# Expert stage of a two-layer decoder trunk: blocks of 1792 columns, 7 KB pieces and eight raw tiles in place of blocks of 896, 3.5 KB pieces and six

## The chip, the core and the metric

The kernel runs on one core of one Trainium2 chip. The metric is the device time of one execution in microseconds. TensorE does the matrix products, ScalarE (ACT) and VectorE (DVE) the element-wise work, GpSimd (POOL) some of the routing and the indirect transfers, and SyncE (SP) issues the loads of the weights. Sixteen DMA engines move the data.

## What is computed

Two decoder layers on 256 tokens of width 1024, all in float32. The first has a gated convolution beside windowed attention, then a dense SwiGLU. The second has block attention (with 256 tokens it is causal attention on one block), then an expert SwiGLU: eight experts with 3584 hidden columns, each token sent to two. Both end with a per-layer embedding. The change is in the expert stage:

```python
def swiglu(x, w_gate, w_up, w_down):
    return (jax.nn.silu(x @ w_gate) * (x @ w_up)) @ w_down

def moe_swiglu(x, w_router, w_gate, w_up, w_down):
    logits = (x @ w_router).astype(jnp.float32)
    top_vals, top_idx = lax.top_k(logits, TOP_K)
    top_w = jax.nn.softmax(top_vals, axis=-1)
    gates = jnp.sum(jax.nn.one_hot(top_idx, N_EXPERTS, dtype=jnp.float32) * top_w[..., None], axis=-2)
    out = jnp.zeros_like(x)
    for e in range(N_EXPERTS):
        out = out + gates[..., e:e + 1].astype(x.dtype) * swiglu(x, w_gate[e], w_up[e], w_down[e])
    return out
```

An expert has three matrices of 1024 x 3584 floats, 14.68 MB each, so that the stage reads 8 x 3 x 14.68 = 352 MB.

## The kernel before

Experts are handled in pairs ("duos"), four of them with these inputs. Of a duo one job is **wide** (up to 128 tokens) and one **small** (up to 64). The wide job's products are made of three: its weights and its inputs are split into a high part in float32r and the rest, and TensorE adds high x high, high x low and low x high. ScalarE makes the high part of a weight tile (`w_hi`, L1096), VectorE the low one (`w_lo`, L2486), so a wide tile passes through both before TensorE has it. The small job uses the raw float32 tile as it was loaded, and since its result has only 64 rows, two products lie side by side on the two halves of the array (`tile_position`).

**Tiles and slots.** SyncE loads weight tiles into `raw`, six slots of up to 1 MB, one after the other in a fixed order, and waits for the slot's last reader ahead of each (`slot_free`): of a wide tile that is VectorE's low part (`lo_made`), of a small one TensorE's products (`tile_used`). There are four `w_hi` buffers and three `w_lo` buffers. L421 is the line of all these loads.

**Blocks.** The 3584 hidden columns are worked in four blocks of 896 (`CUT`). A step of 24 tiles has, in this order of tile numbers: four gate tiles of the wide job (0 to 3), its four up tiles (4, 6, 8, 9) with two down tiles of the small job's last block between them (5, 7), the small job's gate tiles (10, 11, 13, 15) with its other down tiles (12, 14), and then in turn four down tiles of the wide job (16, 18, 20, 22) and four up tiles of the small one (17, 19, 21, 23). A gate or up tile holds two of the eight 128-row slices of the matrix, 896 columns of each: every partition gets two pieces of 896 x 4 = 3584 bytes, 896 KB in all. A down tile holds 256 rows, and a partition gets two neighbouring rows, one piece of 8192 bytes; the fourth of a block has 128 rows and pieces of 4096.

**Folding.** In a small gate or up tile the two slices are computed on the two array halves (L1839). So the two halves of the result are partial sums that have to be added: ScalarE copies both out (L1116, L1120), TensorE transposes them (`turn_sums`, L1798, seven transposes each for gate and up), ScalarE copies the one part (L1125, L1130), VectorE adds the other (L2504, L2510), and only then come Silu (L1135) and the product (L2516). The small down products (L1887) also have two partial sums, which `fold_y` adds once a duo; the sums stand in two PSUM banks, cleared by VectorE. The wide job's hidden values are transposed with seven transposes a block (`turn_wide`, L1788), split into `hidT_hi` (L1112) and `hidT_lo` (L2498), and used by `wide_down` (L1852) in two banks that `clear_wide` clears.

**Order.** Each engine's order is written out by hand. On ScalarE that is `block`, `second_half`, `final_half`; on VectorE `block`; on TensorE `first_half`, `second_half`, `final_half`; on SyncE `superstep`. Silu of the wide gate sums (L1107) stands on ScalarE behind the splits of tiles 4 and 6, the first two up tiles, once gate tile 3 is used, and the copy of the turned hidden values (L1112) ahead of the split of the first down tile.

**Opening and end.** The first expert's gate and up tiles for the wide job can be loaded before the routing is known; the small job's expert number is read from `job_int` (SP waits for `ids_ready`, L550). At the end the sums of both jobs are scattered back to their tokens with products (`scatter_wide` L1771, `scatter_small` L1781), and the four tiles of `o_ple_gate` follow.

## Time and profile before

| | us |
|---|---|
| three runs, median (lowest to highest) | 1411.6 (1408.15 to 1413.55) |
| the profiled execution, whole | 1411.16 |
| its span, first to last instruction | 1409.4 |
| TensorE busy | 1348.0 (96%) |
| VectorE busy | 769.7 (55%) |
| ScalarE busy | 670.2 (48%) |
| read from HBM | 438.04 MB |

"Busy" is the time in which at least one instruction of an engine ran; a busy TensorE need not be at its peak. The granted clock is the share of TensorE's full clock that the chip gave, 0.993 over the whole run; it has two levels, 2.4 GHz (1.00) and 1.2 GHz (0.50). A time "to landing" runs from the issue of a transfer to the semaphore that says that it is complete, so it holds the wait in the queue too. In the order of time the start of one group and the start of the next give the price of a group better than its own length, since products overlap.

### The profile page before, as it was taken

To read this page: it belongs to the slowest core of one execution; us is meant where nothing else is said; L and a number is where in the kernel's file an instruction comes from. 1 tells how busy PE (TensorE), PEld (TensorE's weight loads), DVE (VectorE), ACT (ScalarE), POOL (GpSimd) and SP (SyncE) were. 2 spreads that over 40 slices of the span, in tenths; PEclk is the share of its full clock that TensorE was granted. 3 is DMA by queue.
4 is the path that set the end of the run, shared out by engine and by line. 5 is a ranking of instruction groups with operands and counts; after the bars stand their busy time and mean duration, and the time that the engine had idled before them with its cause. 6 is when DMAs were issued, how large, how long until landed. Compare 5 with 4: busy or idle time off the path is not lost.

```text
span 1409.4 us, 18620 instructions
## 1 busy us (share of the span) xinstructions
PE 1348.0 (96%) x6863; PEld 962.0 (68%) x6863; DVE 769.7 (55%) x812; ACT 670.2 (48%) x751; POOL 61.8 (4%) x119
## 2 busy tenths in 40 slices
PE   9999999999999998999999999999999999999987
PEld 8988888889997665665655655656556566575545
DVE  5767545467566654463563544645546446364446
ACT  5555444456456345353553443634535445354354
POOL 2000000000000270000000000000000001000000
PEclk9999999999999999999999999999999999999999
DMA  9655555577443899999999999999999999999980
GB/s 324 242 177 185 181 197 189 180 237 232 152 131 109 333 395 394 385 405 384 394 413 379 390 401 384 402 402 376 398 385 401 382 396 410 411 388 401 379 342 30
DMA packets 135588, 447.33 MB, mean 317 GB/s; under 512 B 8410, under 2 KB 30054, under 8 KB 123247
## 3 DMA queue, kind: packets, MB, share of 16 engines
q1 hardware_dynamic: 130560, 430.99, 80.6%
q0 software_dynamic: 3072, 8.91, 1.8%
q10 hardware_dynamic: 1902, 6.71, 1.4%
q8 instruction: 34, 0.56, 0.2%
q14 instruction: 20, 0.16, 0.0%
HBM read 438.04 MB, written 8.54 MB: 317 GB/s over the span
## 4 chain that ended last, share of the span: by engine, by line
PE 69%; DMA 18%; DVE 4%; ACT 4%; issue 3%; SPq 1%; ACTq 0%; DVEq 0%
PE banks L1819 18%; PE banks L1265 16%; DMA raw<-in_o_exp_down 8%; DMA raw<-in_o_exp_gate 8%; PE banks L1839 7%; PE banks L1852 6%; PE banks L1887 5%; PE banks L1299 5%; PE banks L1573 4%; DVE w_lo L2486 2%; ACT w_hi L1096 2%; DMA raw<-in_e_w_in 1%; PE banks L1798 1%; SPq L421 1%; DVE work L2504 1%
## 5 line engine op out<-in xcount | busy, mean ns | idle before, releaser
L2486 DVE TENSOR_TENSOR w_lo<-raw,w_hi 128x1792 fp32r<-128x1792 f32 (+1 forms) x189 | 382.1, 2024 | 276.5 <-ACT w_hi L1096 272.0
L1096 ACT ACTIVATE w_hi<-raw 128x1792 fp32r<-128x1792 f32 (+1 forms) x188 | 319.5, 1700 | 301.3 <-DMA raw<-in_o_exp_down 150.2
L1839 PE MATMUL banks<-raw,scores 128*64 128x448 f32 x1024 | 214.9, 547 | 0.5 <-DMA raw<-in_o_exp_up 0.5
L2033 DVE TENSOR_TENSOR w_lo<-raw,w_hi 128x2048 fp32r<-128x2048 f32 x69 | 157.4, 2289 | 91.3 <-PE banks L1265 49.9
L742 ACT ACTIVATE w_hi<-raw 128x2048 fp32r<-128x2048 f32 x74 | 141.7, 1916 | 130.0 <-PE banks L1265 79.7
L1839 PEld LDWEIGHTS banks<-raw,scores 128*64 128x64 f32 x1024 | 66.5, 136 | 114.4 <-issue 112.4
L1819 PE MATMUL banks<-w_hi,x_hi 128*128 128x448 f32 x512 | 133.7, 383 | 0.0
L1819 PE MATMUL banks<-w_hi,x_lo 128*128 128x448 f32 x512 | 126.5, 369 | 0.0
L1819 PE MATMUL banks<-w_lo,x_hi 128*128 128x448 f32 x512 | 126.3, 368 | 0.1
L1819 PEld LDWEIGHTS banks<-w_hi,x_hi 128*128 128x128 f32 x512 | 91.2, 190 | 38.5 <-issue 21.8
L1887 PE MATMUL banks<-raw,work 128*64 128x512 f32 x448 | 109.0, 603 | 0.0
L1265 PE MATMUL banks<-w_hi,x_lo 128*128 128x512 f32 (+1 forms) x304 | 108.5, 357 | 0.3 <-DVE x_lo L2068 0.3
L1265 PE MATMUL banks<-w_hi,x_hi 128*128 128x512 f32 (+1 forms) x304 | 108.1, 356 | 0.0
L1265 PE MATMUL banks<-w_lo,x_hi 128*128 128x512 f32 (+1 forms) x304 | 108.1, 356 | 0.0
L1819 PEld LDWEIGHTS banks<-w_lo,x_hi 128*128 128x128 f32 x512 | 95.7, 189 | 10.9 <-DVE w_lo L2486 1.9
L1819 PEld LDWEIGHTS banks<-w_hi,x_lo 128*128 128x128 f32 x512 | 97.3, 190 | 8.5
L1112 ACT ACTIVATE m_hi<-banks 128x896 fp32r<-128x896 f32 x16 | 14.7, 919 | 172.7 <-PE banks L1788 172.7
L1852 PE MATMUL banks<-w_hi,m_hi 128*128 128x512 f32 x224 | 70.0, 429 | 17.4 <-ACT w_hi L1096 17.4
L1852 PEld LDWEIGHTS banks<-w_hi,m_hi 128*128 128x128 f32 x224 | 37.7, 190 | 63.4 <-ACT w_hi L1096 44.0
L1852 PE MATMUL banks<-w_lo,m_hi 128*128 128x512 f32 x224 | 66.8, 412 | 3.8 <-DVE w_lo L2486 3.7
L1265 PEld LDWEIGHTS banks<-w_hi,x_lo 128*128 128x128 f32 x304 | 57.4, 189 | 8.8 <-DVE x_lo L2068 0.7
L1852 PE MATMUL banks<-w_hi,m_lo 128*128 128x512 f32 x224 | 63.4, 396 | 0.0
(339 smaller groups left out, 1715.8 us busy)
## 6 DMA issues: line engine op xcount, KB each, us to landing
raw<-in_o_exp_gate SPq DMA_DIRECT2D x128, 896.0 KB, 7.9
raw<-in_o_exp_up SPq DMA_DIRECT2D x128, 896.0 KB, 9.2
raw<-in_o_exp_down SPq DMA_DIRECT2D x96, 1024.0 KB, 8.9
raw<-in_o_exp_down SPq DMA_DIRECT2D x32, 512.0 KB, 8.4
raw<-in_o_w_qkv SPq DMA_DIRECT2D x12, 1024.0 KB, 5.9
raw<-in_e_ffn_gate SPq DMA_DIRECT2D x11, 1024.0 KB, 5.2
raw<-in_e_ffn_up SPq DMA_DIRECT2D x11, 1024.0 KB, 5.2
raw<-in_e_ffn_down SPq DMA_DIRECT2D x11, 1024.0 KB, 4.9
```

Source lines behind the costliest of these rows:

```text
L742: act.activation(w_hi[:, at % HI, 0:size], raw[:, at % RAW, 0:size], ACT.Copy).then_inc(hi_made, 1)
L1096: act.activation(w_hi[:, (MOE_T + w) % HI, 0:size], raw[:, (MOE_T - SKIP + i) % RAW, 0:size], ACT.Copy).then_inc(hi_made, 1)
L1112: act.activation(hidT_hi, turned.rearrange("p (c t) -> p c t", t=P), ACT.Copy).then_inc(hidT_hi_made, 1)
L1265: mm = pe.matmul(dst, stat_hl[a], mov_hl[b], start=start and i == 0, stop=stop and i == 2)
L1299: mm = pe.matmul(dst, both(w, ALL, k, slice(f * P, (f + 1) * P))[s], both(XHL, ALL, k)[m], start=start and (k, i) == (0, 0), stop=(k, i) = ...
L1573: mm = pe.matmul(bank[4 + b][:, :], (ffn_hi, ffn_lo)[s][parity][:, c + kk, t * P:(t + 1) * P], w[m][:, kk, half * HALF:(half + 1) * HALF], ...
L1819: mm = pe.matmul(bank[first + f][:, 0:CUT // 2], x[:, 2 * k + kk, 0:P], w[:, kk, f * (CUT // 2):(f + 1) * (CUT // 2)], start=start and kk ...
L1839: mm = pe.matmul(bank[first + f][kk * SMALL:(kk + 1) * SMALL, 0:CUT // 2], x_small[:, 2 * k + kk, :], w[:, kk, f * (CUT // 2):(f + 1) * (C ...
L1852: mm = pe.matmul(bank[6 + half], (hidT_hi, hidT_lo)[s][:, 2 * k + kk, :], w[m][:, kk, half * HALF:(half + 1) * HALF], start=False, stop=en ...
L1887: return pe.matmul(bank[4 + half][at * SMALL:(at + 1) * SMALL, :], hid_rows[:, 2 * k + kk, :], w[:, kk, half * HALF:(half + 1) * HALF], st ...
L2033: ve.tensor_tensor(w_lo[:, at % LO, 0:size], raw[:, at % RAW, 0:size], w_hi[:, at % HI, 0:size], ALU.subtract)\
L2486: ve.tensor_tensor(w_lo[:, (MOE_T + w) % LO, 0:size], raw[:, (MOE_T - SKIP + i) % RAW, 0:size], w_hi[:, (MOE_T + w) % HI, 0:size], ALU.sub ...
```

## The change

- `UP` = 1792 is now the width of a block, and there are two of them instead of four. A step has 48 tiles. A gate or up tile holds one 128-row slice, 1792 columns of it: one piece of 7168 bytes for a partition, 896 KB in all as before. Down tiles are as before.
- The tiles of a step come in longer runs: eight wide gate tiles (0 to 7), eight small down (8 to 15), eight wide up (16 to 23), eight small gate (24 to 31), four wide down (32 to 35), eight small up (36 to 43), four wide down (44 to 47).
- In small gate and up tiles the two array halves now take the two halves of the columns instead of the two slices. Nothing has to be folded: Silu and the product work on the sums, and seven transposes (`turn_hid`) turn the hidden values once. The small down products put the two halves of the output columns on the array halves and start their bank anew in each step; VectorE copies or adds the sums to `y_s` (`small_sums`).
- There are eight raw slots (`RING`): the two new ones lie where `x_lo` and the two halves of the layer embedding (`p_hi`, `p_lo`) were, and become free when the router's products are done, and when the last tile ahead of the stage is used.
- The wide gate takes four banks, the wide up the same four later, so that the wide up waits for Silu. The order on each engine is written anew.

SyncE's order, and who has to let go of a slot:

```diff
 CUT = 7 * P
-BLOCKS = D_FFE // CUT
+UP = 2 * CUT
+BLOCKS = D_FFE // UP
+RING = (2, 3, 4, 5, 0, 1, 6, 7)
+STEP_TILES = 48
+SKIP = 8
+WIDE_AT = (*range(0, 8), *range(16, 24), *range(32, 36), *range(44, 48))
...
-            eg = o_exp_gate[0].rearrange("e (c p) (b n) -> e b p c n", p=P, n=CUT)
-            eu = o_exp_up[0].rearrange("e (c p) (b n) -> e b p c n", p=P, n=CUT)
+            eg = o_exp_gate[0].rearrange("e (c p) (b n) -> e b p c n", p=P, n=UP)
+            eu = o_exp_up[0].rearrange("e (c p) (b n) -> e b p c n", p=P, n=UP)
...
+                was = i - len(RING)
                 if j is None and was < SKIP:
+                    if i - SKIP < RAW:
+                        sp.wait_ge(lo_made, MOE_T - RAW + (i - SKIP) + 1)
+                    elif i - SKIP == RAW:
+                        sp.wait_ge(logitT_ready, 1)
+                    else:
+                        sp.wait_ge(tile_used, MOE_T)
                     return
...
-                load_part(w[e, of, :, 2 * k:2 * k + 2], i, j, b, final)
+                for k in range(KC):
+                    load_part(w[e, of, :, k:k + 1], at + k, j, b)
...
+            def second_part(wide, small, of, j, b):
+
+                up(eg, small, of, 24, j, b)
+                down(wide, of, range(4), 32, j, b)
+                up(eu, small, of, 36, j, b)
+                down(wide, of, range(4, 8), 44, j, b)
+
+            def superstep(wide, of, small_was, of_was, small, j, b):
+
+                up(eg, wide, of, 0, j, b)
+                down(small_was, of_was, range(8), 8, j, b)
+                up(eu, wide, of, 16, j, b)
+                second_part(wide, small, of, j, b)
```

ScalarE and VectorE:

```diff
-            def gate_copy():
-                act.activation(in_halves(gate_s), gate_out, ACT.Copy).then_inc(s_copied, 1)
-            def high_gate(j, b):
-                act.wait_ge(fold_ready, 2 * step_no(j, b, 0) - 1)
...
+            def second_part(j, b, turn_next=False, placing=False):
+
+                for w in range(16, 20):
+                    next_wide(w, j, b)
+                turned_wide(j, b)
+                used(31, j, b)
+                silu_small()
+                for w in range(20, 24):
+                    next_wide(w, j, b)
...
+            def step_of(b, j, first=False, final=False):
+
+                next_wide(4, j, b)
...
+                turned_small(steps_done(j, b))
+                for w in range(5, 11):
+                    next_wide(w, j, b)
+                used(7, j, b)
+                silu_wide(j, b)
+                next_wide(11, j, b)
...
+            def small_sums(used_no, keep=None):
+
+                ve.wait_ge(tile_used, used_no + 1)
+                if keep is not None:
+                    ve.wait_ge(y_stored, 48 * keep + 32)
+                    ve.tensor_copy(y_s, bank[4]).then_inc(s_y_made, 1)
+                else:
+                    ve.tensor_tensor(y_s, y_s, bank[4], ALU.add).then_inc(s_y_made, 1)
...
+            ve.wait_ge(tile_used, tile_at(47, last, 1) + 1)
+            gate_low(0)
+            gate_low(1)
+            small_sums(tile_at(STEP_TILES + 7, last, 1))
+            gate_low(2)
             scattered()
```

TensorE:

```diff
+            def small_up(k, i, j, b):
                 for f in range(2):
-                    for kk in range(2):
-                        mm = pe.matmul(bank[first + f][kk * SMALL:(kk + 1) * SMALL, 0:CUT // 2], x_small[:, 2 * k + kk, :],
-                                       w[:, kk, f * (CUT // 2):(f + 1) * (CUT // 2)], start=k == 0, stop=k == 3,
-                                       tile_position=(0, kk * SMALL), skip_group_check=True)
+                    for half in range(2):
+                        mm = pe.matmul(bank[4 + f][half * SMALL:(half + 1) * SMALL, 0:CUT // 2], x_small[:, k, :], w[:, 2 * half + f],
+                                       start=k == 0, stop=k == KC - 1, tile_position=(0, half * SMALL), skip_group_check=True)
...
+            def second_part(j, b, start, stop, turn_next=False, final=False):
+                s = steps_done(j, b)
+                for k in range(KC):
+                    small_up(k, 24 + k, j, b)
+                    if k == 1:
+                        turn_wide(0, j, b)
+                    if k == 2:
+                        turn_wide(1, j, b)
+                for k in range(4):
+                    wide_down(k, 32 + k, j, b, start, stop)
+                pe.wait_ge(s_silu_made, s + 1)
+                for k in range(KC):
+                    small_up(k, 36 + k, j, b)
...
+                for k in range(4, 8):
+                    if final and k == 6:
+                        turn_hid(s + 1)
+                    wide_down(k, 40 + k, j, b, start, stop)
+
+            def step_of(b, j, first=False, final=False):
+                s = steps_done(j, b)
+                pe.wait_ge(hidT_lo_made, 2 * s)
...
+                for k in range(KC):
+                    if k == 2:
+                        turn_hid(s)
+                    wide_up(0, k, k, j, b)
+                pe.wait_ge(s_hidT_made, s)
+                for k in range(8):
+                    small_down(k, 8 + k, j, b)
...
+                pe.wait_ge(e_silu_made, 2 * s + 2)
+                for k in range(KC):
+                    wide_up(0, k, 16 + k, j, b)
+                pe.wait_ge(s_y_made, s)
+                second_part(j, b, start=first, stop=not first, turn_next=not first and not final, final=final)
```

How the instructions stand. **ScalarE around Silu of the wide gate sums.** `tile_loaded` with a number is the semaphore of that raw slot; `w_hi<-raw` is the split of a tile. Before (Silu is L1107):

```order
L1089 ISA
L1096 ACTIVATE w_hi<-raw 128x1792 [waits tile_loaded4,tile_used]
L1089 ISA
L1107 ACTIVATE work<-banks 128x896 [waits hidT_ready,tile_used]
L1089 ISA
L1095 ISA [waits tile_used]
L1096 ACTIVATE w_hi<-raw 128x1792 [waits tile_loaded0]
```

In the change (Silu is L1085, now two of 896 columns):

```order
L1075 ACTIVATE w_hi<-raw 128x1792 [waits tile_loaded2]
L1068 REGISTER_ALU
L1075 ACTIVATE w_hi<-raw 128x1792 [waits tile_loaded3,tile_used]
L1068 REGISTER_ALU
L1075 ACTIVATE w_hi<-raw 128x1792 [waits tile_loaded4,tile_used]
L1068 REGISTER_ALU
L1085 ACTIVATE work<-banks 128x896 [waits tile_used]
L1085 ACTIVATE work<-banks 128x896
```

Slots 2, 3 and 4 hold tiles 16, 17 and 18 here: three up tiles, which come behind eight small down tiles, are split ahead of Silu. Before, these were the first two up tiles (slot 4 holds tile 6 here), and one small down tile lies between them and the gate tiles.

**ScalarE around the copy of the turned hidden values** (L1091 in the change; tiles 32 to 35 are in slots 2 to 5, the last of 1024 columns):

```order
L1075 ACTIVATE w_hi<-raw 128x2048 [waits tile_loaded2]
L1068 REGISTER_ALU
L1075 ACTIVATE w_hi<-raw 128x2048 [waits tile_loaded3,tile_used]
L1068 REGISTER_ALU
L1075 ACTIVATE w_hi<-raw 128x2048 [waits tile_loaded4,tile_used]
L1068 REGISTER_ALU
L1075 ACTIVATE w_hi<-raw 128x1024 [waits tile_loaded5,tile_used]
L1090 ISA
L1091 ACTIVATE m_hi<-banks 128x896 [waits hidT_ready]
L1090 REGISTER_ALU
L1091 ACTIVATE m_hi<-banks 128x896 [waits hidT_ready]
```

Before, the copy (L1112) stood ahead of the split of the first down tile; now all four down tiles are split ahead of it.

**TensorE in the first wide gate tiles of a step.** Before, both sets of sums are turned here:

```order
L1819 MATMUL banks<-w_lo,x_hi 128x448 x3
L1798 MATMUL banks<-cst,scores 128x128 [waits s_copied]
L1798 MATMUL banks<-cst,scores 128x128 x6
L1282 REGISTER_ALU
L1819 MATMUL banks<-w_hi,x_hi 128x448 [waits hi_made]
L1819 MATMUL banks<-w_hi,x_hi 128x448 x3
L1819 MATMUL banks<-w_hi,x_lo 128x448 x4
L1819 MATMUL banks<-w_lo,x_hi 128x448 [waits lo_made]
L1819 MATMUL banks<-w_lo,x_hi 128x448 x3
L1798 MATMUL banks<-cst,bias 128x128 [waits s_gate_added]
L1798 MATMUL banks<-cst,bias 128x128 x6
```

In the change one set of seven, and in a step of twice the columns:

```order
L1753 MATMUL banks<-w_lo,x_hi 128x448 [waits lo_made]
L1753 MATMUL banks<-w_lo,x_hi 128x448 x3
L1733 MATMUL banks<-cst,work 128x128 [waits s_hid_made]
L1733 MATMUL banks<-cst,work 128x128 x6
L1220 REGISTER_ALU
L1753 MATMUL banks<-w_hi,x_hi 128x448 [waits hi_made]
L1753 MATMUL banks<-w_hi,x_hi 128x448 x7
L1753 MATMUL banks<-w_lo,x_hi 128x448 [waits lo_made]
L1753 MATMUL banks<-w_lo,x_hi 128x448 x3
```

The turn of the up sums with its wait is gone. (High x high and high x low stand together here, since both inputs are now parts of `x_hi`'s buffer.)

## Rows read from the trace of the kernel before

**Rows 1.** Table by stretch: from:to, length, busy us (instructions), clock, DMA share, GB/s.
```profile
600.00:1300.00 700.00, 666.74 (x3128) 416.19 (x3127) 360.33 (x254) 325.70 (x294) 13.70 (x13) 1.00 1.01 395
```
**Rows 2.** DMA issues of the page: count, KB each, median us to landing.
```profile
raw<-in_o_exp_gate SPq DMA_DIRECT2D x128, 896.0 KB, 7.9
raw<-in_o_exp_down SPq DMA_DIRECT2D x32, 512.0 KB, 8.4
...
raw<-in_e_ffn_down SPq DMA_DIRECT2D x11, 1024.0 KB, 4.9
```
**Rows 3.** Order of time, TensorE: third wide gate tile, 14 steps apart.
```profile
506.51 1.06 PE L1819 MATMUL banks<-w_hi,x_hi 128*128 128x448 f32 x4
...
1306.06 1.06 PE L1819 MATMUL banks<-w_hi,x_hi 128*128 128x448 f32 x4
```
**Rows 4.** Order of time, TensorE, inside one step: start us, us, what, count.
```profile
849.85 0.99 PE L1819 MATMUL banks<-w_hi,x_hi 128*128 128x448 f32 x4
...
852.33 0.99 PE L1819 MATMUL banks<-w_hi,x_hi 128*128 128x448 f32 x4
...
854.90 1.94 PE L1887 MATMUL banks<-raw,work 128*64 128x512 f32 x8
...
856.77 1.07 PE L1819 MATMUL banks<-w_hi,x_hi 128*128 128x448 f32 x4
...
866.32 3.23 PE L1839 MATMUL banks<-raw,scores 128*64 128x448 f32 x16
...
869.48 1.10 PE L1788 MATMUL banks<-cst,work 128*128 128x128 f32 x7
...
883.98 1.18 PE L1852 MATMUL banks<-w_hi,m_hi 128*128 128x512 f32 x4
...
886.91 1.72 PE L1839 MATMUL banks<-raw,scores 128*64 128x448 f32 x8
```
**Rows 5.** SP's DMA queue at 832:840, 1339:1343, 1355:1358: packets, MB, engines' share.
```profile
q1 hardware_dynamic: 964, 3.25, 102.7%
...
q1 hardware_dynamic: 236, 1.67, 99.7%
...
q1 hardware_dynamic: 294, 1.16, 100.1%
```
**Rows 6.** Groups by line and shape, 480 to 1300: count, busy us, mean ns, idle before.
```profile
L1096 ACT ACTIVATE w_hi<-raw 128x1792 fp32r<-128x1792 f32 x114 | 193.9, 1700 | 140.7 <-DMA raw<-in_o_exp_gate 68.7 <-DMA raw<-in_o_exp_up 66.0 <-PE banks L1819 4.8
...
L1798 PE MATMUL banks<-cst,bias 128*128 128x128 f32 x98 | 15.6, 299 | 18.5 <-DVE work L2504 18.5
...
L1107 ACT ACTIVATE work<-banks 128x896 f32<-128x896 f32 x14 | 12.9, 922 | 3.3 <-PE banks L1819 3.1
```
**Rows 7.** TensorE after idling (idle us in brackets), and the clock granted then.
```profile
1190.42 1.10 PE L1798 MATMUL banks<-cst,bias 128*128 128x128 f32 x7 [2.27 <-DVE work L2504]
...
1191.00:1195.00 4.00, 4.00 (x16) 3.60 (x15) 3.96 (x4) 1.06 (x3) 3.05 (x2) 0.57 1.03 418
...
1345.67 2.07 PE L1852 MATMUL banks<-w_hi,m_hi 128*128 128x512 f32 x4 [3.72 <-ACT w_hi L1096]
...
1345.00:1352.00 7.00, 6.33 (x18) 5.05 (x19) 5.97 (x4) 6.08 (x5) 0.00 (x0) 0.51 1.01 419
```
**Rows 8.** Order of time at the opening, TensorE and SyncE's issues.
```profile
449.97 0.97 PE L1819 MATMUL banks<-w_hi,x_hi 128*128 128x448 f32 x4
...
462.41 3.68 PE L1748 MATMUL banks<-work,xn 128*128 128x64 f32 x32
...
462.87 2.34 SPq L421 DMA_DIRECT2D raw<-in_o_exp_gate  x4
```
**Rows 9.** Order of time at the end: last down loads, both scatters.
```profile
1333.75 17.24 SPq L421 DMA_DIRECT2D raw<-in_o_exp_down  x8
...
1364.58 3.70 PE L1771 MATMUL banks<-work 128*128 128x512 f32 x8
...
1372.64 2.84 PE L1781 MATMUL banks<-work 128*128 128x512 f32 x6 [1.64 <-ACT work L1251]
```

724 lines of the change are left out of this document (271 added, 453 removed).

## The prediction

> **What bounds the kernel now.** I read the table by stretch first, then the times to landing of the DMA issues, then the queue in short stretches, then the order of time. The expert stage reads 8 x 3 x 14.68 = 352 MB. Over 700 us of it the 16 DMA engines are busy 1.01 of the time at 395 GB/s, while TensorE is busy 667 of 700 us, VectorE 360 and ScalarE 326 [rows 1]. So the queue of transfers is the bound and TensorE stands close behind. Loads land some 8 us after their issue, against 4.9 us for one of 1 MB in the dense stage [rows 2]: they wait for each other in the queue. A block of 24 tiles returns every (1306.06 - 506.51) / 14 = 57.1 us [rows 3].
>
> TensorE's own work, start to start [rows 4]: a wide gate or up tile 852.33 - 849.85 = 2.48 us, a small gate or up tile (869.48 - 866.32) / 2 = 1.58, seven transposes 1.1, a small down tile 856.77 - 854.90 = 1.87 (half of that for a tile of one chunk), a wide down tile 886.91 - 883.98 = 2.93, the half one 1.5. A block is 8 x 2.48 + 8 x 1.58 + 6.5 + 10.3 + 1.1 + 2.2 (14 transposes of sums) = 52.5 us of 57.1. The rest is waiting for data.
>
> **Transfers: pieces of 7168 B.** Only gate and up tiles change: the same bytes in half the packets. Stretches in which one kind of tile moves alone give a price per packet [rows 5]. Gate and up: 1.027 x 8 us x 16 engines = 131.5 us for 3.25 MB / 3584 B = 907 packets, 145.0 ns. Down: 0.997 x 4 x 16 = 63.8 us for 1.67 MB / 8192 B = 204 packets, 313 ns. The line through both is 14.3 ns for the packet and 36.5 ns for each 1000 B, so 275.7 ns for 7168 B against 290 for two of 3584 B. Bounds: at the full rate of the 8192 B packets it is 274 ns (16 saved). On the other side the 4096 B packets of 1355 to 1358 take 48.0 us / 283 = 170 ns, 24.1 B/ns, which is worse than 24.7 for 3584 B; at that rate 7168 B take 297 ns, 7 more than now. So -7 to +16 ns for a pair, and I am near the upper end since both pure stretches are long and quiet, and the third has a load from GpSimd's queue in it. A tile saves 128 x 14.3 / 16 = 0.114 us. Of 256 such tiles 24 come in the opening, where TensorE sets the pace (below); 232 x 0.114 = **26.5 us less** (bounds -13 to +30).
>
> The Trainium skill (DMA: Bandwidth & Descriptors, section Why small descriptors are slow (HBM only)) gives a fixed overhead of some 3 cycles a packet beside one for each 32 B, which is an estimated 1.3% of 538 us, 7 us instead of 26.5. The rows show a larger fixed part, 14 of 145 ns.
>
> **Folding.** For 1792 columns, 28 transposes of sums (4 groups, 1.1 us each, 15.6 us for 14 groups [rows 6]) become 7; two clearings and the waits at the sums go. That is some 3.3 us of TensorE per 48 tiles, and copies and adds on ScalarE and VectorE, which are busy about half the time [rows 1]. None is on the path, because the queue is the bound: worth **0** by itself. It is the cover for the next part. TensorE's sum for 48 tiles becomes: A, eight wide gate tiles and the turn 20.9; B, eight small down 13.1; C, eight wide up 19.8; D, eight small gate and two turns 14.8; E, four wide down 10.3; F, eight small up 12.6; G, four wide down 10.3. That is 101.8 us, against 114.2 - 32 x 0.114 = 110.5 us of transfers.
>
> **Longer runs of one kind, eight raw tiles.** ScalarE does its queue in order, and two things now stand behind loads. Silu stands behind the splits of tiles 16, 17 and 18, so C begins 1.70 + 2 x 0.92 = 3.5 us after tile 18 has landed; the copy of the turned hidden values stands behind the split of tile 35 (1024 columns, so some 1.70 x 1024 / 1792 = 1.0), and E begins 1.0 + 0.9 = 2 us after tile 35 [rows 6]. Behind each wait are queued TensorE's C and E, and SyncE's loads that need the slots these free. I follow one step from the landing of tile 18 (0), with transfers of 110.5 us for 48 tiles (2.31 us a gate tile, 2.6 a down tile). C runs 3.5 to 23.3, D to 38.1. Tile 35 lands at 39.2, so E runs 41.2 to 51.5, F to 64.1, G to 74.4, the next A to 95.3, B to 108.4, and tile 18 lands at 110.5. TensorE idles 3.1 us before E and 5.6 before C. Does a slot come too late? Tile 32 goes out when D's first tile is used, at 24.9, and the queue lasts until 30.0; tile 44 at 53.1, queue until 57.6; tile 16 at 97.2, until 103.7. A lone load needs 4.9 us, 2.5 of it its transfer [rows 2, 5], so it has to be issued 2.4 us ahead. Margins are 2.7, 2.1 and 4.2 us: the queue stays full, but by little.
>
> **The clock** eats of these margins. After TensorE had idled 2.27 us at 1188 it was granted 0.57 of its clock for the next 4 us, that is mostly the 1.2 GHz level, and after 3.72 us at 1342 it was granted 0.51 over 7 us [rows 7]. A stretch of 3.4 to 7 us at half speed costs 1.7 to 3.5 us. Both new idles are of that size. The later tile 32 then misses by -1.0 to +0.8 us and tile 44 by -0.4 to +1.4. I take 0.5 us a step, **4 us more** over 7.5 steps (0 to 15). The Trainium skill (TensorE: Matmul & The Clock Gate, section What's actually happening) says that the low clock is the default and that activity lifts it; by this trace it agrees, and by that rule both waits of every step would be followed by the low level.
>
> **Opening and end.** Before, four loads wait until 462.87 for the number of the expert [rows 8]; afterwards that number is wanted only after 16 wide tiles. But those 16 are TensorE's: 449.97 + 16 x 2.48 + 3.7 (gathering for the small job) + 1.3 (the first hidden product: 0.9 as for other operations on 896 columns, and two handovers) = 494.7 [rows 6, 8]. Tile 32 is issued at 496.3 and lands at 501.2, tile 35 at 508. By then 16 gate or up tiles (37.1 us of transfers) and 4 down tiles (8.8) more than the first eight are in; before, from 462.9 + 1.3 to 508 there are 43.8 us of transfers. **2 us less** (-3 to +5). At the end the last down tile, issued at 1351, has landed by about 1359, and the last scatter begins at 1372.64, 13.6 us later [rows 2, 9]. Afterwards TensorE ends G some 6.5 us before the last landing (74.4 + 4, for hidden values that come later, against 66.8 + 18.3 = 85.1), and has eight small tiles 13.1, the scatter of the wide rows 3.7 and an addition of 0.7 with some 0.7 of handovers ahead of it: 11.7 us. **2 us less** (-4 to +4, since this addition stands on VectorE behind two tiles of the next stage).
>
> **Sum.** The profiled execution took 1411.2 us (span 1409.4), 0.4 under the median 1411.6 of the three runs. 1411.2 - 26.5 + 4 - 2 - 2 = 1384.7, so **1384 us**, 27 less.
>
> **Rivals.**
> (1) The packets are no cheaper per byte. For: the 4096 B row. Then 1411.2 + 4 - 4 = 1411, and with 7 ns more for each pair, 1424; a gain of half the forecast's, 1398. Against: two quiet stretches differ by 6% in bytes per ns. I give 0.2, most of it between 1398 and 1412. (By the rule of the Trainium skill above it is 1404.)
> (2) The queue runs dry at tiles 32 and 44. The mechanism is the one above: ScalarE's order holds TensorE until tile 18 and tile 35 have landed, the clock halves after both, and TensorE frees slots too late. It is decided at a delay of 2 to 3 us in C or E, and above 4 us lost in a step (30.5 us of gains over 7.5 steps) the change is slower. At 6 us it is 1384 + 7.5 x 5.5 = 1425. For: the margins of 2.1 and 2.7 us, and the two idles. Against: TensorE has 8.9 us of slack a step, and the waits come when D and F, which take less than their loads, have caught up. 0.12.
> (3) A part of that, 1 to 3 us a step: 1388 to 1403. 0.1.
> (4) The forecast, 1374 to 1392: 0.58.
>
> **How the numbers follow.** A measurement of this kernel can tell some 0.5%, 7 us, from no change. Faster than 1404.5: cases 4 and 3 and a third of 1, 0.74. Within: most of the rest of 1, 0.13. Slower than 1418.7: case 2 and the far end of 1, 0.13. The range runs from 1371 (packets at the full rate, no clock loss, the quiet end of the tail) to 1410, which leaves out the worse half of 1 and all of 2.
>
> **What would show it.** In the profile after: DMA share near 1.0 through the stage and some 404 GB/s in place of 395; pure gate stretches near 276 ns a packet (if 290, rival 1). The 48-tile period near 110.5 us; if it is above 112 with a DMA share under 0.97, rival 2, and SyncE's waits then name TensorE's small up or down line. TensorE idle a few us twice a step, behind Silu and behind the copy of the turned values, with the half clock after them. TensorE's busy time lower by some 25 us. Wrong altogether it would be if the pieces of 7168 B came as two packets each.

## The result, and the profile after

The changed kernel takes 1406.8 us (median), the kernel before 1413.4 in the same comparison: a ratio of 0.9946 with a 95% interval of 0.9926 to 0.9965, so 0.5% faster (7.6 us by the ratio), where 27 us were forecast. One run of the changed kernel, at 2587 us, was a slow one and is not in the ratio. The profiled execution took 1409.0 us, with a span of 1407.3 against 1409.4 before. It is one of the longer ones: the other runs of the changed kernel go from 1397.8 to 1415.4 us, and those of the kernel before from 1408.2 to 1417.1.

From the table by stretch (from:to, length, busy us of TensorE, its weight loads, VectorE, ScalarE, GpSimd, then the granted clock, the DMA share, GB/s), the row that answers to [rows 1]:

```profile
600.00:1300.00 700.00, 638.93 (x3013) 432.63 (x3013) 336.03 (x216) 284.97 (x235) 14.78 (x13) 0.96 0.99 395
```

The same 395 GB/s as before, and 404 were forecast. TensorE is 28 us less busy, its clock is 0.96 instead of 1.00. The page's queues and its issues of loads (count, KB each, median us to landing) answer to [rows 2]:

```profile
q1 hardware_dynamic: 97792, 430.99, 79.4%
...
q8 instruction: 58, 0.95, 0.3%
...
raw<-in_o_exp_gate SPq DMA_DIRECT2D x128, 896.0 KB, 11.0
raw<-in_o_exp_up SPq DMA_DIRECT2D x128, 896.0 KB, 8.1
raw<-in_o_exp_down SPq DMA_DIRECT2D x96, 1024.0 KB, 10.4
```

The loads have the packets that were announced: 97,792 for the same 430.99 MB, where the page of before has 130,560. New are 58 packets of instructions, 34 before. A step of 48 tiles shows in TensorE's order of time, by the start of the wide up tiles (C) of the first and the seventh step; in brackets is the idle time just before and what ended it:

```profile
585.62 1.11 PE L1753 MATMUL banks<-w_hi,x_hi 128*128 128x448 f32 x2 [5.53 <-ACT work L1085]
...
1270.13 1.86 PE L1753 MATMUL banks<-w_hi,x_hi 128*128 128x448 f32 x4 [5.04 <-ACT work L1085]
```

(1270.13 - 585.62) / 6 = 114.1 us a step, within 0.1 us of the 2 x 57.1 of [rows 3]; the forecast was 110.5. So in this execution nothing of the cheaper packets has come through (one at the median would be some 0.3 us a step shorter), and the question is what keeps the step at 114.1. TensorE's waits from 490 to 1350 (line, what it waited for, us in total, times, longest):

```profile
PE banks L1753 <- ACT work L1085: 32.4, 7, 6.1
PE banks L1790 <- ACT m_hi L1091: 22.1, 8, 5.1
PE banks L1790 <- DVE w_lo L2377: 6.2, 6, 2.1
PE banks L1753 <- issue: 5.8, 1, 5.8
PE banks L1753 <- ACT w_hi L1075: 4.2, 2, 3.8
```

L1085 is Silu, before C: 32.4 / 7 = 4.6 us each. L1091 is the copy of the turned hidden values, before the wide down tiles (E): 22.1 / 8 = 2.8 us each. Both were forecast (5.6 and 3.1). The last two rows were not.

### The profile page after: what moved, and what is told of

It reads as the page before. It is cut to its first block, busy times and chain, and to the rows that moved or that the text cites. A ratio compares the mean times of both kernels' runs of the same rounds, so it can differ in the third digit from the quotient of the medians.

```text
span 1407.3 us, 17891 instructions
## 1 busy us (share of the span) xinstructions
PE 1312.6 (93%) x6687; PEld 979.1 (70%) x6687; DVE 741.7 (53%) x766; ACT 626.2 (44%) x679; POOL 62.4 (4%) x119
## 3 DMA queue, kind: packets, MB, share of 16 engines
q1 hardware_dynamic: 97792, 430.99, 79.4%
## 4 chain that ended last, share of the span: by engine, by line
PE 73%; DMA 14%; ACT 4%; issue 4%; DVE 3%; SPq 1%; ACTq 0%; DVEq 0%
PE banks L1753 23%; PE banks L1203 15%; PE banks L1778 8%; PE banks L1790 7%; DMA raw<-in_o_exp_down 6%; PE banks L1237 5%; PE banks L1511 4%; DMA raw<-in_o_exp_up 4%; PE banks L1815 3%; DMA raw<-in_o_exp_gate 2%; ACT w_hi L1075 2%; DMA raw<-in_e_w_in 1%; PE banks L1726 1%; SPq L421 1%; ACT work L1085 1%
## 5 line engine op out<-in xcount | busy, mean ns | idle before, releaser
L1075 ACT ACTIVATE w_hi<-raw 128x1792 fp32r<-128x1792 f32 (+2 forms) x188 | 316.9, 1701 | 505.5 <-DMA raw<-in_o_exp_down 306.1
L1753 PE MATMUL banks<-w_hi,x_hi 128*128 128x448 f32 x1024 | 247.8, 387 | 42.7 <-ACT work L1085 32.4
L1753 PEld LDWEIGHTS banks<-w_hi,x_hi 128*128 128x128 f32 x1024 | 203.4, 200 | 68.9 <-issue 44.7
L1778 PE MATMUL banks<-raw,scores 128*64 128x448 f32 x1024 | 200.4, 543 | 1.2 <-DVE work L2386 1.2
L720 ACT ACTIVATE w_hi<-raw 128x2048 fp32r<-128x2048 f32 x70 | 133.9, 1916 | 127.3 <-PE banks L1203 79.7
L1778 PEld LDWEIGHTS banks<-raw,scores 128*64 128x64 f32 x1024 | 70.3, 137 | 112.0 <-issue 110.5
L1753 PEld LDWEIGHTS banks<-w_lo,x_hi 128*128 128x128 f32 x512 | 100.5, 197 | 11.2 <-DVE w_lo L2377 1.2
L1815 PE MATMUL banks<-raw,scores 128*64 128x512 f32 x448 | 98.8, 595 | 0.0
L1790 PE MATMUL banks<-w_hi,m_hi 128*128 128x512 f32 x224 | 66.9, 417 | 23.2 <-ACT m_hi L1091 22.1
L1815 PEld LDWEIGHTS banks<-raw,scores 128*64 128x64 f32 x448 | 31.1, 137 | 60.6 <-issue 60.4
L1790 PEld LDWEIGHTS banks<-w_hi,m_hi 128*128 128x128 f32 x224 | 42.7, 198 | 43.7 <-ACT w_hi L1075 29.3
L1203 PEld LDWEIGHTS banks<-w_hi,x_lo 128*128 128x128 f32 x304 | 57.5, 189 | 8.9 <-DVE x_lo L1959 0.7
L1203 PEld LDWEIGHTS banks<-w_lo,x_hi 128*128 128x128 f32 x304 | 57.5, 189 | 8.1
L1203 PEld LDWEIGHTS banks<-w_hi,x_hi 128*128 128x128 f32 x304 | 57.5, 189 | 8.0
```

What stands on the lines that cost most here:

```text
L720: act.activation(w_hi[:, at % HI, 0:size], raw[:, at % RAW, 0:size], ACT.Copy).then_inc(hi_made, 1)
L1075: act.activation(w_hi[:, (MOE_T + w) % HI, 0:size], ring[RING[i % len(RING)]][:, 0:size], ACT.Copy).then_inc(hi_made, 1)
L1203: mm = pe.matmul(dst, stat_hl[a], mov_hl[b], start=start and i == 0, stop=stop and i == 2)
L1753: mm = pe.matmul(bank[first + f][:, 0:CUT // 2], x[:, k], w[:, f], start=start, stop=stop)
L1778: mm = pe.matmul(bank[4 + f][half * SMALL:(half + 1) * SMALL, 0:CUT // 2], x_small[:, k, :], w[:, 2 * half + f], start=k == 0, stop=k == K ...
L1790: mm = pe.matmul(bank[6 + half], (hidT_hi, hidT_lo)[s][:, c0 + kk, :], parts[m][:, kk, half * HALF:(half + 1) * HALF], start=begin and kk ...
```

## One step, forecast against trace

The step that begins with the landing of tile 18 at 923.32 (the split of it starts there), order of time on ScalarE, TensorE and SyncE:

```profile
918.90 1.70 ACT L1075 ACTIVATE w_hi<-raw 128x1792 fp32r<-128x1792 f32 x1 [19.20 <-DMA raw<-in_o_exp_up]
...
923.32 1.70 ACT L1075 ACTIVATE w_hi<-raw 128x1792 fp32r<-128x1792 f32 x1 [0.49 <-DMA raw<-in_o_exp_up]
924.92 1.71 ACT L1085 ACTIVATE work<-banks 128x896 f32<-128x896 f32 x2
...
926.75 3.35 PE L1753 MATMUL banks<-w_hi,x_hi 128*128 128x448 f32 x8 [6.11 <-ACT work L1085]
...
947.92 2.10 PE L1778 MATMUL banks<-raw,scores 128*64 128x448 f32 x10
...
949.69 7.33 SPq L421 DMA_DIRECT2D raw<-in_o_exp_down  x4
...
964.92 1.18 PE L1790 MATMUL banks<-w_hi,m_hi 128*128 128x512 f32 x4 [2.40 <-ACT m_hi L1091]
...
976.58 4.98 SPq L421 DMA_DIRECT2D raw<-in_o_exp_down  x4
...
1003.66 1.11 PE L1753 MATMUL banks<-w_hi,x_hi 128*128 128x448 f32 x2 [5.75 <-issue]
...
1028.40 0.33 SPq L421 DMA_DIRECT2D raw<-in_o_exp_up  x1
```

| after the landing of tile 18, us | forecast | trace |
|---|---|---|
| C starts | 3.5 | 3.4 |
| C ends | 23.3 | 24.6 |
| tile 32 is issued | 24.9 | 26.4 |
| E starts | 41.2 | 41.6 |
| tile 44 is issued | 53.1 | 53.3 |
| next A starts | 74.4 | 80.3 |
| next tile 16 is issued | 97.2 | 105.1 |

The mechanism of the forecast is there, nearly to the microsecond, up to the next A. C takes 21.2 us in place of 19.8, since it starts mostly at the 1.2 GHz level (0.52 over 923 to 930 below; over the seven steps C takes 21.7 on average, from 21.2 to 22.4). Then comes something that isn't in the forecast: at 997.9 TensorE has ended G, the tiles of A have landed (the first was split at 994.00), and it starts only at 1003.66, with "issue" as the cause and again at two thirds of its clock. The slots come so late that the queue stands empty from 1026 to 1029:

```profile
923.00:930.00 7.00, 3.25 (x9) 2.90 (x10) 4.51 (x3) 6.54 (x12) 0.00 (x0) 0.52 1.02 418
1003.60:1011.00 7.40, 7.33 (x25) 6.63 (x26) 2.03 (x1) 1.71 (x1) 0.00 (x0) 0.66 1.02 419
...
1026.00:1029.00 3.00, 3.00 (x15) 1.02 (x15) 0.00 (x0) 0.00 (x0) 0.00 (x0) 1.00 0.10 41
```

In all steps together the trace has ten places at which the DMA engines are more than half idle for 0.75 to 3.5 us: the opening, and one or two in each step. Before it had one.

## The experiments

All ratios are against the kernel before, from the runs of the same comparison. A difference between two kernels is given in us of 1413; by the intervals of the two ratios it is good to 3 to 5 us.

**Both of ScalarE's moves.** Silu is taken ahead of the splits of tiles 16 to 18, the turned copy ahead of those of tiles 32 to 35.

```diff
 def second_part(...):
+    turned_wide(j, b)
     for w in range(16, 20):
         next_wide(w, j, b)
-    turned_wide(j, b)
...
 def step_of(...):
-    for w in range(5, 11):
+    for w in range(5, 8):
         next_wide(w, j, b)
     used(7, j, b)
     silu_wide(j, b)
-    next_wide(11, j, b)
+    for w in range(8, 12):
+        next_wide(w, j, b)
```

> The changed kernel with two moves in ScalarE's program: Silu stands right behind the split of tile 7's successor (wide tile 7 of the step), ahead of the splits of tiles 16 to 18, and the copy of the turned hidden values stands ahead of the splits of tiles 32 to 35. Theory A (ScalarE's order holds TensorE, TensorE frees slots late, the queue runs dry; the dry time and the slow 8192-byte packets around it are the lost gain): TensorE's idle times before C and before E (3 to 6 us and 2 to 5 us a step) go, the time with under 0.3 MB outstanding falls from 18 us to under 6, idle time of the DMA engines from 28 to about 14 us, half-clock stretches from 16 to under 8, and the time to 1384 to 1392. Theory B (the dry spots come from TensorE's own pace, its code loads at the loop's two back-jumps and its half clock, whoever waits for what): 1400 to 1407, idle moves elsewhere. Theory C (the 8192-byte packets are slower because the transfers now come in longer runs of one kind, whatever is outstanding; 337 ns in place of 322): idle falls but those packets stay at 337 ns, time 1393 to 1399.

Measured: 1380.0 us, 0.9755 (0.9741 to 0.9769), 27.0 us less than the changed kernel. The table by stretch:

```profile
600.00:1300.00 700.00, 654.61 (x3098) 433.17 (x3096) 341.64 (x221) 296.15 (x241) 12.54 (x13) 0.97 1.00 409
```

Two starts of C in the order of time, five steps apart:

```profile
579.69 1.08 PE L1754 MATMUL banks<-w_hi,x_hi 128*128 128x448 f32 x4 [0.35 <-ACT w_hi L1075]
...
1133.40 0.87 PE L1754 MATMUL banks<-w_hi,x_hi 128*128 128x448 f32 x3
```

A step takes (1133.40 - 579.69) / 5 = 110.7 us, the forecast's 110.5, and the time is 4 us under the forecast's 1384. That is theory A, even below its range of 1384 to 1392. B falls for most of the loss. C falls too: packets of 8192 bytes take 319 ns on average here, 338 in the changed kernel, at the same run lengths. Half-clock stretches went from 15 to 11 only, so that number of the expectation (under 8) was wrong.

**Each move alone.**

> Only Silu is moved ahead of the splits of tiles 16 to 18. Theory A: the idle before C (3 to 6 us a step) goes, that before E (2.3 to 5 us) stays; a half to two thirds of the gain of both moves, 1391 to 1400. Theory B: within 3 us of the changed kernel.

Measured: 1398.3 us, 0.9885 (0.9858 to 0.9913): 9 us of the 27. TensorE's wait before E grew, from 22.1 us in total to 55.1 (from 490 to 1350, as above):

```profile
PE banks L1791 <- ACT m_hi L1091: 55.1, 8, 9.6
```

> Only the copy of the turned hidden values is moved ahead of the splits of tiles 32 to 35. Theory A: the idle before E goes, that before C stays or grows, since C waits for tile 18 in any case; a quarter to a half of the gain of both, 1397 to 1404. Theory B: within 3 us of the changed kernel.

Measured: 1393.8 us, 0.9852 (0.9836 to 0.9868): 13 us of the 27, below the expected 1397. The wait before C stays (32.4 us in the changed kernel):

```profile
PE banks L1753 <- ACT work L1085: 33.7, 7, 6.5
```

So the copy before E, which I had taken for the smaller one, is at least as large as Silu: by the intervals the 5 us between the two runs are barely more than their uncertainty. The two together bring 27 us where the sum is 22, which is within the uncertainty of four runs (some 6 us). That one wait feeds the other shows in the trace instead: with Silu alone moved, TensorE comes to E earlier and waits there 33 us longer.

**Shorter packets in the changed kernel.** The loads take a pair of chunks of 896 columns.

```diff
-eg = o_exp_gate[0].rearrange("e (c p) (b n) -> e b p c n", p=P, n=UP)
+eg = o_exp_gate[0].rearrange("e (q c p) (b n) -> e b q p c n", p=P, c=2, n=UP // 2)
...
-        load_part(w[e, of, :, k:k + 1], at + k, j, b)
+        load_part(w[e, 2 * of + k // 4, k % 4], at + k, j, b)
```

> The changed kernel, but each gate and up load takes a pair of chunks of 896 columns instead of one chunk of 1792: the same bytes of the same block into the same slot in packets of 3584 bytes, so the products are of wrongly placed weights. All else stays. If the packet price is what the traces of before and after say (2 x 148 ns against 279), 256 tiles x 128 x 16.5 / 16 ns = 34 us more transfers; some of it is taken up by what is now idle (28 us), so 1420 to 1437. If the time of the changed kernel is set by TensorE's waits and not by its transfers: under 1415. If the packets of 7168 bytes bring nothing when all else is equal: 1407, with the packet times of a pair at 279.

Measured: 1412.1 us, 0.9994 (0.9978 to 1.0010), 7 us more than the changed kernel, not 13 to 30. It lies under 1415, the second case: what sets the time of the changed kernel is in the main TensorE's waits and not its packets.

**The same with both moves.**

> The kernel with both of ScalarE's moves, and gate and up loads in packets of 3584 bytes (pairs of chunks of 896 columns in place of one of 1792; the products are of wrongly placed weights). With both moves the DMA engines are busy nearly all the time. If the packet price is what the traces say (2 x 145 to 148 ns against 279), the 232 tiles behind the opening take 232 x 128 x 11 to 17 / 16 ns = 20 to 31 us longer: 1400 to 1411. If a pair costs no more than one long packet once the queue is full: 1380 to 1385. In the changed kernel, where the queue ran dry anyway, the same edit cost 5 us.

Measured: 1396.5 us, 0.9880 (0.9864 to 0.9897), 17.7 us more than with long packets; just under the range. From 620 to 740, short packets with both moves:

```profile
620.00:740.00 120.00, 111.25 (x522) 74.26 (x523) 62.11 (x43) 53.50 (x51) 3.11 (x4) 0.97 1.02 406
```

Long packets with both moves:

```profile
620.00:740.00 120.00, 113.01 (x534) 76.78 (x534) 60.60 (x41) 52.16 (x51) 3.10 (x4) 0.96 1.02 415
```

With a queue that is full the long packets raise the rate of all transfers, down tiles included, by 415 / 406, 2.2%. With the same short packets the kernel before moved 397 GB/s from 620 to 740, and 395 from 600 to 1300 [rows 1], at a DMA share of 1.01.

**Long packets alone, in the kernel before.**

```diff
-eg = o_exp_gate[0].rearrange("e (c p) (b n) -> e b p c n", p=P, n=CUT)
+eg = o_exp_gate[0].rearrange("e (g c p) (b n) -> e g c p b n", p=P, c=2, n=2 * CUT)
...
-    load_part(w[e, of, :, 2 * k:2 * k + 2], i, j, b, final)
+    load_part(w[e, of, k // 2, :, k % 2:k % 2 + 1], i, j, b, final)
```

> The kernel before with one part of the change alone: its gate and up loads take one chunk of 1792 columns in place of two chunks of 896, so packets of 7168 bytes, in the order and at the times of before (the products are of wrongly placed weights). With a full queue 7168-byte packets moved 416 GB/s and 3584-byte ones 407 (the two kernels with both moves), 2.2% of some 840 us: 16 to 18 us. If the transfers bound the kernel before, 1392 to 1399; by the price a packet that the prediction took (26.5 us) 1385 to 1389. If TensorE and the waits bound it as much (it moved 397 GB/s with 3584-byte packets where 407 was to be had, with 2.1 MB outstanding against 3.4), 1400 to 1410.

Measured: 1404.3 us, 0.9931 (0.9910 to 0.9953), 9.7 us less than before: the third case. The main term of the prediction, taken alone and put into the very kernel from whose trace it was worked out, brings 10 us and not 26.5:

```profile
600.00:1300.00 700.00, 666.17 (x3151) 420.21 (x3149) 364.81 (x256) 330.18 (x298) 12.87 (x13) 1.00 1.00 398
```

**Fewer slots.** A load waits in addition for the tile seven (or six) places back.

```diff
 was = i - len(RING)
+if j is not None:
+    kind = lambda n: n % STEP_TILES in WIDE_AT
+    if kind(was) or not kind(i - LIMIT):
+        was = i - LIMIT
```

> The changed kernel with a load held until the tile seven before it is free, not eight (but for the first wide tile after small ones). The prediction put the margin of tiles 32, 44 and 16 at 2.7, 2.1 and 4.2 us; one slot less takes 2.3 to 2.6 us of each. If the margins were as small as the dry spots say: 1414 to 1428. If the number of slots isn't what the changed kernel lacks: 1404 to 1410.

Measured: 1449.8 us, 1.0253 (1.0223 to 1.0282), 43 us more for one slot, twice what the worst case said (1428, 21 us).

> The kernel of both_rotated with a load held until the tile six before it is free (but for two tiles after small ones): six slots as before the change, in place of eight. If the deeper queue is a gain of its own (3.4 MB outstanding against 2.1 before, 407 against 397 GB/s with packets of the same size), it falls back: 1388 to 1405. If two slots fewer only cost at the few tiles with a small margin: 1374 to 1385.

Measured: 1412.4 us, 0.9982 (0.9964 to 1.0000), 38 us more than the kernel it was made from (below) and above the range. The stretch 600 to 1300 with seven slots in the changed kernel:

```profile
600.00:1300.00 700.00, 617.50 (x2876) 414.44 (x2875) 316.04 (x205) 271.87 (x226) 13.95 (x13) 0.94 0.96 376
```

With six in the kernel with the turned loop:

```profile
600.00:1300.00 700.00, 640.82 (x3002) 424.74 (x3000) 330.55 (x215) 288.40 (x236) 12.62 (x13) 0.96 0.99 395
```

Why one slot costs so much shows when the traces are counted by how much is outstanding, that is the bytes that SyncE has issued less the bytes that have moved. From 520 to 1300 us, GB/s (and us spent there):

```
MB outstanding              under 1     1 to 2      2 to 3      over 3
before (3584 B)             384 (40)    392 (296)   395 (362)   403 (82)
both moves, short packets   177 (16)    399 (38)    405 (124)   408 (602)
changed kernel (7168 B)     299 (40)    381 (200)   403 (228)   416 (312)
seven slots                 254 (107)   384 (237)   398 (232)   418 (204)
both moves                  212 (18)    399 (49)    412 (151)   417 (562)
```

Full and empty are no two states. The rate is lower by degrees: from 417 over 3 MB to 381 to 399 between 1 and 2 MB, while the share of busy DMA engines still reads 0.98 to 1.01, and it falls off below that. Against 417 GB/s throughout, the rows make (an estimate) 71 us of the 780 lost with seven slots, 37 in the changed kernel, 25 of these between 1 and 3 MB, and 13 with both moves. The differences, 34 and 24 us, are most of the 43 and 27 that were measured. This is a count and not an experiment: with the same packets and 1 to 2 MB outstanding the changed kernel moves 381 GB/s and the one with both moves 399, so the amount isn't all that matters.

**TensorE kept busy in its waits.**

```diff
+def keep_busy(at, times):
+    for _ in range(times):
+        pe.matmul(bank[at], zeros_r[:, :], xw_hi[:, 0:4], start=False, stop=False)
...
+    keep_busy(6, 16)
     pe.wait_ge(e_silu_made, 2 * s + 2)
...
+    if j is not None:
+        keep_busy(7, 9)
     for k in range(4):
         wide_down(k, 32 + k, j, b, start, stop)
```

> The changed kernel with ScalarE's order as it was, and TensorE kept busy in its two waits of a step: 16 products with a block of zeros (512 columns each) before C and 9 before E, added to the sum of the down products as zeros. Theory E (the half clock behind the waits is a large part of the loss: 16 stretches of 3.4 or 6.8 us, 78 us in all at half speed, which is up to 39 us of TensorE's work): the half-clock stretches fall to under 8 and the time to 1390 to 1399. Theory A (the loss is the late start behind ScalarE, the clock adds little to it): 1402 to 1412, with fewer half-clock stretches and the same dry spots. The added code is 50 instructions a step.

Measured: 1394.6 us, 0.9854 (0.9823 to 0.9885), 13 us less than the changed kernel, with ScalarE's order as it was. Theory E holds as well. The clock of the stretch is 0.99:

```profile
600.00:1300.00 700.00, 670.13 (x3225) 453.47 (x3224) 341.85 (x221) 294.03 (x242) 16.18 (x13) 0.99 1.00 401
```

In its trace six half-clock stretches with 24 us are left of 15 with 78 us. C takes 19.7 us in six of seven steps. The clock's part of the loss and the late starts' part overlap, since some of the half clock comes with the late starts (15 stretches with 78 us, 11 with 55 with both moves). No run has both remedies, so the 13 and the 27 us can't be added.

**TensorE's back-jump.** With both moves the trace has just three places of 0.5 us or more, up to 1320 us, at which the DMA engines stand more than half idle: the opening, and 3.5 and 4.0 us, some 28 us behind the start of each wait at the back-jump of the loop. One of them begins with this wait of TensorE, in the order of time:

```profile
990.54 0.74 PE L1754 MATMUL banks<-w_hi,x_hi 128*128 128x448 f32 x1 [5.44 <-ACT w_hi L1075]
```

The clock behind it, and the empty queue, by stretch:

```profile
990.50:1000.00 9.50, 9.46 (x37) 8.63 (x38) 3.67 (x2) 2.61 (x3) 0.00 (x0) 0.71 1.01 419
...
1013.00:1017.00 4.00, 4.00 (x20) 1.46 (x20) 0.00 (x0) 1.73 (x2) 0.00 (x0) 1.00 0.22 58
```

The split named as the cause is that of the fourth tile of A, for which the first tile doesn't wait. What lies there is a packet of 16 KB on the queue of instructions, at 987.7 us. Between two back-jumps of the changed kernel (774 to 1002) that queue carries

```profile
q8 instruction: 10, 0.16, 0.3%
```

160 KB, while the kernel before fetched nothing from 689 to 1175. So I take it that the loop's body of two unrolled steps doesn't stay where TensorE reads its instructions from, and that each jump back waits for a new fetch. The Trainium skill (Advanced Engine Details and Errata, section ISA Cache) gives TensorE 128 KB in lines of 16 KB; the trace agrees, with packets of 16,384 bytes and a body of ten of them, which is more than 128 KB. To test it TensorE's loop is turned: it begins with E to G of the step before, so that the jump stands before E. The order of the work stays.

```diff
+small_gate(None, None)
 with pe.Fori(0, last) as j:
-    step_of(1, j)
-    step_of(2, j, first=True)
-step_of(1, last, final=True)
+    second_part(j, 0, start=True, stop=False)
+    first_part(1, j)
+    second_part(j, 1, start=False, stop=True, turn_next=True)
+    first_part(2, j, first=True)
+second_part(last, 0, start=True, stop=False)
+first_part(1, last)
+second_part(last, 1, start=False, stop=True, final=True)
```

> Both moves, and TensorE's loop turned so that its back-jump stands before the wide down tiles (E) and not before the wide gate tiles (A); the order of its work is the same. In the trace with both moves the queue runs dry for 4.0 and 3.5 us, 27 us after each of the two back-jumps, where TensorE had idled 6.3 and 5.4 us with a packet of 16 KB of instructions under way. Theory D (code loads at the back-jump delay A, the slots that it frees and so the queue): the idle moves to E, where TensorE waits some 3 us for data anyway, the two dry spots go or halve, 1373 to 1378. Rival (the idle at the back-jump is absorbed, and the dry spots belong to the tile order, as in the steps between): 1379 to 1382, dry spots as before.

Measured: 1372.8 us, 0.9714 (0.9700 to 0.9728), 5.8 us less than with both moves, at the lower end of theory D's range. The wait stands before E now, where TensorE waited for data anyway, and the two empty spots are gone (one of 1.5 us came). So the wait goes where the jump goes; that it is the fetch that ends it rests on the packets beside it. The first of the two waits, in the order of time:

```profile
727.11 1.21 PE L1791 MATMUL banks<-w_hi,m_hi 128*128 128x512 f32 x2 [4.79 <-issue]
```

The table by stretch:

```profile
600.00:1300.00 700.00, 659.04 (x3131) 433.62 (x3128) 343.03 (x223) 299.87 (x243) 11.64 (x13) 0.97 1.01 414
```

**Less work for TensorE.** Does TensorE still set the pace there? The products of the inputs' low parts with the weights' high parts are left out of the wide tiles.

> The kernel of both_rotated without the products of the inputs' low parts with the weights' high parts in the wide tiles (a third of TensorE's work there: a wide tile takes 1.65 us in place of 2.48). A step then moves 44.0 MB; at the 416 GB/s of the full queue that is 105.9 us, against 109.1 us from C to C now. If what is left above the transfers is TensorE's lateness, 1345 to 1360. If the queue's own pace is the bound already, 1365 to 1372.

Measured: 1364.9 us, 0.9652 (0.9621 to 0.9682), 8.8 us less, for 77 us less of TensorE's busy time in 700:

```profile
600.00:1300.00 700.00, 582.42 (x2534) 337.24 (x2530) 345.49 (x223) 301.23 (x245) 12.10 (x13) 0.92 1.01 415
```

415 GB/s against 414: in the loop of the kernel with the turned loop the transfers are the bound, as the forecast had wanted them. 1364.9 lies at the edge of the second case. A step takes 108.9 us here and 109.1 in the kernel with the turned loop; the 105.9 us of my expectation had left out what the other queues move. So the loop gives 1 to 2 of the 8.8 us. 4.6 lie in the opening, where TensorE sets the pace: the first C starts at 574.45 in place of 579.06.

**The end of the last step.** In addition VectorE multiplies the small job's hidden values before it adds gathered rows.

> The kernel of both_rotated with one more move: in the last step VectorE multiplies the small job's hidden values before it adds the second half of the gathered rows to h, not after. TensorE waited 4.95 us for these at the end with both moves, 3 us of it for the additions. If the chain to the last scatter is TensorE's, 2.5 to 3.5 us less than both_rotated: 1370 to 1375. If the gate tiles of the next stage end last, no change.

Measured: 1371.7 us, 0.9716 (0.9699 to 0.9733), no difference to the kernel with the turned loop: inside the first case's range, but without its gain. The waits in its trace, TensorE's:

```profile
1303.36 1.71 PE L1734 MATMUL banks<-cst,work 128*128 128x128 f32 x7 [2.08 <-DVE work L2406]
...
1328.71 1.98 PE L1720 MATMUL banks<-work 64*128 64x512 f32 x6 [2.65 <-DVE work L2415]
```

The wait for the hidden values fell from 5.0 us to 2.1, and the one for the last sum is now 2.65, 0.79 in the kernel with both moves: VectorE's additions were moved onto the next thing TensorE wants. The best kernel is the one with the turned loop, 2.9% under the kernel before and 2.3% under the change.

## Why the prediction was wrong

The direction was right and the size wrong by a factor of four. The step that cost most is "the queue stays full, but by little", with its 4 us for the clock: the place of two operations in ScalarE's order, and the late starts, late slots and half clock behind it, cost 27 us. Point by point:

- **What bounds the kernel before.** This step failed first. From a DMA share of 1.01 I took it that the queue of transfers is the bound. From 620 to 740 the same short packets moved 406 GB/s with more outstanding (both moves), and 397 in the kernel before, which had 2 MB outstanding on average. Long packets alone brought 9.7 us. So the transfers were only one part of what set its pace. I take the rest to be how soon the six slots came round; but TensorE was busy 667 of 700 us there, and no run gave the kernel before more slots or less work for TensorE, so which of the two it was stays open.
- **The price of a packet, 26.5 us.** As a duration it was right: 279 ns measured, 275.7 forecast, 2 x 148 before. What it brings depends on what else holds the slots: 7 us in the changed kernel, 9.7 in the one before, 17.7 where the queue is full. Even there it is less than the mean durations in those two traces say (2 x 145.3 against 277.9 ns, an estimated 24 us for 232 tiles); why isn't shown. By the Trainium skill (DMA: Bandwidth & Descriptors, section Why small descriptors are slow (HBM only)) it was 7 us, which is too little for the full queue.
- **Eight raw tiles.** The prediction counted the slots only in its margins and gave them no term. With the order mended, six slots instead of eight cost 38 us. That is as much as the gain of the best kernel over the one before (40 us), but it is the price in the new order of tiles with its long runs of one kind; what eight slots are worth in the old order no run shows.
- **The step, and the margins of 2.7, 2.1 and 4.2 us.** The times of C, E and of tiles 32 and 44 came out within 1.5 us. The reading of them failed: "the queue stays full, but by little" took any lead above the 2.4 us of a lone load as good. (Its 404 GB/s doesn't go with its step of 110.5 us either: 395 x 114.2 / 110.5 is 408, and with both moves it is 409.) The table of rates says that a queue with 1 to 2 MB left is already slower by 4 to 9%, and the changed kernel spent 200 us there and 40 below.
- **The clock, 4 us.** Sized by only what exceeded the margins. Keeping TensorE busy gave back 13 us. C took 1.4 to 2.6 us more than its 19.8, at the low end of the forecast's 1.7 to 3.5 for a stretch or under it; it should have been charged in full to the slots. The number of stretches, 15 in seven and a half steps, is the forecast's two a step, but they lie elsewhere: behind all seven waits before C, behind only three of the eight before E (of 2.6, 5.1 and 2.9 us; the five of 1.9 to 2.5 us had none behind them), and the others behind the wait for G's last tile (up to 2.1 us), the back-jumps and the last step's turn. So the prediction's "both waits of every step would be followed by the low level" held for C and not for E.
- **Code loading** was missing altogether. The order of instructions had shown that TensorE's loop went from one block at a time to two unrolled steps. Moving the jump to a place where TensorE waited anyway was worth 5.8 us with both moves.
- **Opening.** The idle time forecast at tile 32 is there, 3.5 us at 497. From 440 to 508 us SP's queue moves 20.2 MB, 20.6 before, and by 550 it is 37.1 against 36.1: 1 us behind, then some 2 us ahead, of which the step's own gain is a part. I put it at nothing to 1 us in place of 2.
- **End.** The last down tile is issued at 1345.4, 5.6 us earlier than in [rows 9], and the last scatter begins at 1368.52, 4.1 us earlier, so the end costs 1.5 us more rather than 2 less (the row is below); the span is only 2.1 us shorter, with a stretch of 3.4 us at half clock from 1373.8. TensorE had no lead of 6.5 us there; that the waits of the steps before had used it up is my reading. TensorE, order of time:

```profile
1368.52 1.98 PE L1719 MATMUL banks<-work 64*128 64x512 f32 x6 [0.79 <-DVE work L2408]
```

- **Folding**, worth 0 by the prediction: no run tells it apart. TensorE is 28 us less busy in 700, but that holds the new order and the waits as well.
- **Luck.** With both moves the time (1380.0) and the step (110.7) come within 4 us and 0.2 us of the forecast, and yet its sum isn't confirmed. This kernel is 34.6 us under the one before; the packets bring 17.7 of them and not 26.5, and the code loads of the back-jumps are still in it. The other 17 come from what the sum put at nothing: the two slots (38 us in the kernel with the turned loop), the order or the folding.
- **The rivals.** The named mechanism of rivals 2 and 3, ScalarE's order and the clock behind it, is what happened, shown by two moves in ScalarE's program. At 27 us over 7.5 steps it is 3.6 us a step, between the 1 to 3 of rival 3 and the 6 of rival 2. I gave the two 0.22 together, against margins which I had myself worked out to be within a microsecond or two of nothing. Rival 1 (packets no cheaper) is refuted by 406 against 415.

What stays open: what set the pace of the kernel before, what the folding and the order of tiles are worth by themselves, why packets of 8192 bytes have a longer mean in the changed kernel (338 ns, with a median of 309; 323 in the kernel before, which had less outstanding, and 319 with both moves), and why the rate is graded. That the 16 engines finish their parts of a load at different times, so that the quick ones run dry first, would explain the graded rate. The Trainium skill (DMA: Bandwidth & Descriptors, section Why a DMA increments its semaphore by 16 and not by 1) says that the engines finish independently; no run here tells the engines apart.

## What to carry to other kernels

A DMA share near 1 doesn't say that the queue is the bound: look at GB/s beside the best stretch of the same packets, and at how many bytes are outstanding. If the rate is under that of the best stretch, as it was here (397 against 406), something else sets a part of the pace, and a cheaper packet brings only a part of its price (9.7 of 26.5 us). When an edit puts an instruction of an in-order engine behind waits for data, count what it holds back in slots, charge the half clock behind a wait in full, and try first whether the instruction can stand ahead of those waits, which here was worth nearly four times the edit itself. And when a loop is unrolled further, look at where the instructions of its busiest engine come from at the jump back.

## What the runs showed of the hardware

- The transfer rate is graded with what is outstanding: with 7168-byte packets 299 GB/s under 1 MB, 381 from 1 to 2, 403 from 2 to 3 and 416 over 3 (the changed kernel), with a DMA share of 0.99 from 600 to 1300; with both moves 399, 412 and 417 from 1 MB up.
- At the jump back over a loop body of ten 16 KB packets of instructions TensorE stood for 3.8 to 6.3 us (changed kernel, `warm`, both moves, turned loop), with a packet of instructions moving beside it; none was fetched in 486 us of the kernel before, and when the jump was moved the wait moved with it.
- Products with a block of zeros in TensorE's waits raise the granted clock: 25 of 512 columns in each step brought it from 0.96 to 0.99 (half clock 24 us in place of 78) and took 13 us off.
- Not every wait of TensorE is followed by the low clock: of the eight before E in the changed kernel the five of 1.9 to 2.5 us weren't, while one of 2.27 us in the kernel before was [rows 7].
- Packets of 7168 bytes raise the rate of a full queue from 406 to 415 GB/s over packets of 3584 bytes (620 to 740, both moves), 17.7 us of the kernel's time.
